# Key-key and key-query products of a delta tile made once and kept for the other scan direction

## The chip, the cores and the metric

The kernel runs on one core of one Trainium2 chip. The metric is the device time of one execution in microseconds (us), lower is better. Engines are named as the profile names them: PE (TensorE matmul), PEld (its weight load), DVE (VectorE), ACT (ScalarE), POOL (GpSimd), SP (SyncE, which issues most transfers). Numbers such as L2178 are lines of the kernel before, unless the text says "of the changed kernel".

## What is computed

One layer of a hybrid backbone: a norm and an input projection, three token mixers side by side (a gated DeltaNet, HGRN2, RG-LRU), an output projection, then a grouped top-2 mixture of 16 experts. There are 128 context tokens and 512 latent tokens. The change touches the DeltaNet alone. Cut to what matters (chunks of the reference are 64 tokens; the kernel handles two at a time, 128 tokens, and gets the same result):

```python
def _gdn_step(S, inp):
    q, k, v, la, beta = inp
    g = jnp.cumsum(la, axis=-1)
    dec = _masked_exp(incl, g[..., :, None] - g[..., None, :])
    lmat = beta[..., :, None] * jnp.einsum('bhid,bhjd->bhij', k, k) * strict   # key-key
    m = jnp.eye(CHUNK) + lmat
    sol = triangular_solve(m, rhs, lower=True, unit_diagonal=True)
    u = sol[..., :GDN_DV] - jnp.einsum('bhck,bhkv->bhcv', sol[..., GDN_DV:], S)
    attn = jnp.einsum('bhik,bhjk->bhij', q, k) * dec                           # key-query
    o = (q * eg) @ S + attn @ u
    S_new = exp(g_end) * S + (k * exp(g_end - g)).T @ u

o_a, st_a = _bidirectional(_gdn_step, s_gdn, (q, k, v, log_alpha[0], beta[0]), (q, k, v, log_alpha[1], beta[1]))
```

Both directions use the same q and k. Only the decays (`dec`) and `beta` differ by direction.

## The kernel before, in words

The 640 tokens are five tiles of 128: tile 0 is the context, tiles 1 to 4 the latents. The delta scan runs in five steps, s = 0 to 4. In each step both directions are worked side by side, four heads each, so that everything comes in eights: the forward direction takes tile `FWD[s]` (0, 1, 2, 3, 4), the backward one tile `BWD[s]` (0, 4, 3, 2, 1). So steps 1 and 4 work on the tiles 1 and 4, steps 2 and 3 on the tiles 2 and 3, with the directions exchanged, and step 0 has tile 0 in both.

The order of the work is written out by hand in `gdn_order()` (L80), and every engine walks through the same list. It is a chain of *levels* that inverts the triangular matrix of step s by doubling (`level`, l = 0 to 5, then the corner blocks `t6` and `d6`), and between the levels one group of eight products is put that belongs to the step before or after. The names of these groups are:

- `gb`: the cumulated decays of the next step (L1098). `wt`: their weighting by beta (L2157, DVE).
- `kk`, key-key products of the next step (L1100), after level 4. DVE multiplies them with the masked decays (L2223 to L2228, four products: two of 64 partitions by 512 elements, two of 64 by 256). The first two give `a_ATc`, of which POOL makes the masks of the next step.
- `kq`, key-query products of the next step (L1102), between `t6` and `d6`. DVE multiplies them with the decays (L2234, one product of 128 by 1024).
- `ks`: keys times state (L1109), after level 5; DVE makes the right side of it (L2249, L2253 twice). `u`: the solution (L1113). `ds`: the state's increment (L1115). `o`: the output (L1122, L1125).

A level is, on PE, products into PSUM (`t1`, two halves of 16 blocks of 64x64), a copy of them by ACT (L1578), products again (`dd`), and a subtraction by DVE (L2178, twice, one for each half). The next level starts with what that subtraction wrote. `level(s, 0)` is on DVE two pairs of products, L2164 (from two SBUF tiles) and L2167 (from SBUF and PSUM). DVE walks its list in order: level 4, `kk` of the next step, level 5, `ks`, `kq` of the next step, level 0 of the next step.

POOL works in order too (L1756 to L1785). For the next step it masks the decays (L1762 twice), copies the step's end decays (L1765 twice), scales queries and keys (L1771 twice, L1777 twice), and then makes six masks of `a_ATc` (L1753 six times), level by level. All of these read and write SBUF.

PSUM has four pairs of banks. The groups of eight products alternate between pairs 2 and 3 (`psum_plan`, L149), in the order of the plan; a group waits until the pair's last user has been read. SP loads rows of the modulation into `xT` after the last use of `xT` as gate weights (L644), then waits for further points of the delta scan, one after the other, before it starts the next transfers.

## Time and profile before

| | |
|---|---|
| runs | 3, median 1076.65 us (1075.40 to 1076.88) |
| span of the profiled execution | 1071.6 us |
| median of the runs less that span | 5.05 us |
| PE busy | 942.1 us (88%) |
| DVE busy | 443.8 us (41%) |
| ACT busy | 257.5 us (24%) |
| POOL busy | 134.6 us (13%) |
| delta scan, about | 427 us to 640 us of the span |

The span goes from the first to the last instruction. The record of the profiled execution has its span and not a time of its own; the 5.05 us are what the timed runs have around such a span. In the rows of a timeline the first number is the start in us from the span's start, the second the time from the first start to the last end of the instructions that the row merges; xN is how many these are; in brackets stands how long the engine was idle before, and who ended that.

### The profile page before, as it was taken

The numbers are of one execution on the slowest core, as the hardware profiler recorded it, in microseconds if no ns is written. First come the engines' busy times: TensorE is split into PE (matmuls) and PEld (weight loads), VectorE is DVE, ScalarE is ACT, GpSimd is POOL, SyncE is SP. The second block draws the span as 40 slices with busy tenths as digits, with TensorE's granted clock in tenths as the row PEclk, the third lists the DMA queues.
The fourth block names the chain that finished last, engine by engine and source line by source line (L and its number), as shares of the span: only waits on it lengthen the run. The fifth ranks groups of instructions, "written<-read, shape, count | busy, mean of one in ns | idle before, by whom it ended". The sixth has DMA issues, their size and how long they took to land.

```text
span 1071.6 us, 23772 instructions
## 1 busy us (share of the span) xinstructions
PE 942.1 (88%) x10749; PEld 655.2 (61%) x10749; DVE 443.8 (41%) x734; ACT 257.5 (24%) x436; POOL 134.6 (13%) x154
## 2 busy tenths in 40 slices
PE   2799998878999889999999799998899999999940
PEld 2554576765665446688999664565858756665510
DVE  1443767974345333465667631555100010100037
ACT  3418233233113227231322310220101101100103
POOL 4000000000003100554246000001000000000021
PEclk9899999989999999999999989988999999999985
DMA  8902008654021900200000247142589999999845
GB/s 297 382 27 79 1 1 316 238 175 147 8 78 61 339 19 1 83 19 22 2 3 23 78 179 313 60 177 94 211 304 386 398 403 383 398 394 395 347 156 195
DMA packets 55772, 192.60 MB, mean 180 GB/s; under 512 B 7323, under 2 KB 10834, under 8 KB 51570
## 3 DMA queue, kind: packets, MB, share of 16 engines
q1 hardware_dynamic: 42096, 161.09, 39.7%
q0 software_dynamic: 6736, 22.81, 6.6%
q10 hardware_dynamic: 6834, 7.11, 1.9%
q8 instruction: 87, 1.43, 0.6%
q14 instruction: 19, 0.16, 0.0%
HBM read 168.27 MB, written 22.73 MB: 178 GB/s over the span
## 4 chain that ended last, share of the span: by engine, by line
PE 74%; DVE 11%; DMA 6%; ACT 4%; issue 4%; ACTq 1%; DVEq 0%; SPq 0%; POOLq 0%
PE ps L731 16%; PE ps L1199 14%; PE ps L1222 7%; PE ps L1019 6%; PE ps L1072 6%; PE ps L721 4%; PE ps L1007 4%; PE ps L976 3%; DMA ring<-in_moe_w_up 2%; PE ps L870 2%; PE ps L821 2%; PE ps L748 2%; DMA ring<-in_ada_w 1%; PE ps L1140 1%; PE ps L967 1%
## 5 line engine op out<-in xcount | busy, mean ns | idle before, releaser
L731 PE MATMUL ps<-hT,ring 128*128 128x128 f32 x704 | 194.2, 437 | 1.9 <-ACT hT L1323 1.9
L731 PEld LDWEIGHTS ps<-hT,ring 128*128 128x128 f32 x704 | 106.8, 193 | 83.6 <-issue 80.1
L2440 DVE TENSOR_TENSOR hT<-ps,hT 128x384 f32<-128x384 f32 (+3 forms) x18 | 9.1, 506 | 245.9 <-ACT hT L1641 235.7
L1199 PE MATMUL ps<-ring,arena 128*32 128x128 f32 (+3 forms) x1104 | 87.3, 377 | 2.5 <-DMA ring<-in_moe_w_up 1.3
L1199 PEld LDWEIGHTS ps<-ring,arena 128*32 128x32 f32 (+1 forms) x1104 | 61.1, 118 | 28.5 <-issue 20.4
L1796 POOL DMA_INDIRECT arena<-h_rows,slot_tok x18 | 16.6, 922 | 384.4 <-PE ps L721 229.5
L1199 PE MATMUL ps<-arena 128*32 128x256 f32 (+2 forms) x1056 | 60.8, 387 | 4.4 <-DVE arena L2432 2.7
L1199 PEld LDWEIGHTS ps<-arena 128*32 128x32 f32 x1056 | 46.7, 112 | 19.4 <-issue 5.0
L721 PE MATMUL ps<-ident,arena 128*128 128x128 f32 (+3 forms) x316 | 44.3, 289 | 11.6 <-DVE arena L2207 5.0
L721 PEld LDWEIGHTS ps<-ident,arena 128*128 128x128 f32 (+3 forms) x316 | 39.3, 177 | 20.6 <-issue 7.7
L2178 DVE TENSOR_TENSOR arena<-arena,ps 128x512 f32<-128x512 f32 x50 | 34.4, 688 | 29.5 <-PE ps L1019 28.7
L1641 ACT ACTIVATE hT<-ps 128x384 f32<-128x384 f32 (+3 forms) x18 | 8.1, 449 | 148.8 <-PE ps L1199 148.8
L1222 PE MATMUL ps<-ring,hT 128*32 128x256 f32 (+2 forms) x384 | 41.4, 470 | 0.5 <-ACT hT L1648 0.5
L1222 PE MATMUL ps<-arena,hT 128*32 128x512 f32 (+2 forms) x360 | 39.5, 516 | 2.0 <-ACT hT L1648 2.0
L748 PE MATMUL ps<-ring,st 128*32 128x128 f32 x768 | 28.4, 309 | 13.4 <-DMA ring<-in_ada_w 6.4
L1578 ACT ACTIVATE hT<-ps 128x256 f32<-128x256 f32 x50 | 18.8, 382 | 87.7 <-PE ps L1019 82.7
L1019 PE MATMUL ps<-arena,hT 64*64 64x64 f32 x960 | 38.0, 219 | 0.2 <-DVE arena L2178 0.2
L1019 PE MATMUL ps<-hT,arena 64*64 64x64 f32 x800 | 33.0, 221 | 5.6 <-ACT hT L1578 5.3
L1072 PE MATMUL ps<-ring,hT 128*128 128x512 f32 x80 | 36.1, 594 | 0.4 <-issue 0.4
L1072 PE MATMUL ps<-ring,mixBC 128*128 128x512 f32 x80 | 36.0, 593 | 0.0
L1652 ACT ACTIVATE hT<-ps 128x768 f32<-128x768 f32 (+3 forms) x18 | 13.1, 727 | 94.5 <-PE ps L1222 94.5
L976 PE MATMUL ps<-xT,hT 128*128 128x512 f32 x80 | 34.9, 594 | 0.6 <-DVE ring L2228 0.6
(438 smaller groups left out, 1485.3 us busy)
## 6 DMA issues: line engine op xcount, KB each, us to landing
ring<-in_ada_w SPq DMA_DIRECT2D x12, 2048.0 KB, 11.3
ring<-in_moe_w_gate SPq DMA_DIRECT2D x7, 2048.0 KB, 9.9
arena<-in_moe_w_gate SPq DMA_DIRECT2D x7, 2048.0 KB, 10.7
arena<-in_moe_w_up SPq DMA_DIRECT2D x7, 2048.0 KB, 15.6
arena<-in_moe_w_down SPq DMA_DIRECT2D x7, 2048.0 KB, 20.4
ring<-in_moe_w_up SPq DMA_DIRECT2D x7, 2048.0 KB, 16.5
ring<-in_moe_w_down SPq DMA_DIRECT2D x7, 2048.0 KB, 21.9
ring<-in_w_in SPq DMA_DIRECT2D x6, 2048.0 KB, 12.8
```

Source lines behind the costliest of these rows:

```text
L721: return nc.tensor.transpose(out, in_, ident[0:n, 0:n])
L731: last = mm(out, w[:, k, cols], rhs(k)[:, a:b], start=(k == 0), stop=(k == KD - 1))
L748: last = mm(bank(name)[32 * c:32 * c + 32, 0:P], cs[:, k, :], slab(name)[:, k, P * c:P * c + P], start=(k == 0), stop=(k == KD - 1))
L821: last = mm(bank(name)[:, 0:256], hT[:, k, P * t:P * t + P], hgate_w[:, k, :], start=(k == 0), stop=(k == KD - 1))
L870: last = mm(bank(name)[64 * r:64 * r + 64, at:at + 64], lhs[:, keys:keys + 64], rhs[:, queries:queries + 64], start=True, stop=True)
L976: last = mm(bank(name)[:, 0:512], hT[:, k, P * t:P * t + P], gate_w[:, k, :], start=(k == 0), stop=(k == KD - 1))
L1007: last = mm(bank(name)[:, P * dh:P * dh + P], lhs(dh), rhs(dh), start=True, stop=True)
L1019: last = mm(out[r, 64 * h:64 * h + 64], lhs[r, 4 * g + h, :], rhs(r, 4 * g + h), start=True, stop=True)
L1072: last = mm(bank(name)[:, 0:512], mix(k, t), slab(("out", half))[:, k, :], start=(k == 0), stop=(k == KD - 1))
L1199: last = mm(ps[rows_of(n, g), GU, 512 * i + at:512 * i + at + width], m_xgT[:, b % 2, k, rows_of(n, j)], w[:, k, col:col + width], start=( ...
L1222: last = mm(ps[rows_of(n, g), DN, at:at + width], m_hidT[:, b % 2, first:first + (P if n == 4 else 32)], w[:, f, col:col + width], start=( ...
L2178: TT(out=XX, in0=XX, in1=bank(name)[:, 0:512].rearrange("p (a x) -> p a x", a=2), op=SUB).then_inc(pair_free[pair(name)], 1)
```

## The change

`kk` and `kq` are made on PE in the steps 0, 1 and 2 only. Step 0 makes four products instead of eight, and DVE reads these four for both directions, from PSUM as before. In the steps 1 and 2 all eight are made, and ACT copies them from PSUM into two buffers in `xT` (`a_kk`, `a_kq`: four tiles, four heads, 128 each). From step 1 on DVE reads them there, in the steps 3 and 4 with the directions exchanged. Two new semaphores take the place of the PSUM pair's, and SP's load of the modulation's rows into `xT` now waits for the last use of the two buffers.

```diff
+LAST_PAIR = 2
@@ job_plan
+        elif kind in ("kk", "kq") and s > LAST_PAIR:
+            continue
@@ layer_program
+        a_kk, a_kq = (xTf[:, 2048 * n:2048 * n + 2048].rearrange("p (n h t) -> p n h t", n=NT - 1, h=GH) for n in range(2))
+        def both_ways(kept, s):
+            return kept[:, FWD[s] - 1::NT - 2 * s][:, 0:2]
@@ SP
-                    sp.wait_ge(*full_after(LATE_GATES[-1]))
+                    sp.wait_ge(s_a_kk_used, NT - 1)
+                    sp.wait_ge(s_a_kq_used, NT - 1)
@@ PE
-                    pe.wait_ge(*free_after(("kk", s)))
+                    pe.wait_ge(*(s_a_kk_used, s) if s else free_after(("kk", 0)))
...
-                    eight(name, kT(s), kT(s))
+                    if s <= LAST_PAIR:
+                        eight(name, kT(s), kT(s), 8 if s else 4)
...
-                    eight(name, kT(s), qT(s))
+                    if s <= LAST_PAIR:
+                        eight(name, kT(s), qT(s), 8 if s else 4)
@@ ACT
+                elif kind in ("kk", "kq") and 0 < s <= LAST_PAIR:
+                    act.wait_ge(*full_after(LATE_GATES[-1]))
+                    act.wait_ge(*full_after(name))
+                    A(both_ways(a_kk if kind == "kk" else a_kq, s), bank(name).rearrange("p (d h t) -> p d h t", d=2, h=GH),
+                      ACT.Copy).then_inc(pair_free[pair(name)], 1)
@@ DVE
+            def pair_products(name, kept):
+                s = name[1]
+                if s == 0:
+                    dve.wait_ge(*full_after(name))
+                    return wide(fours_of(bank(name)[:, 0:512]), 1, 2)
+                for n in range(1, min(s, LAST_PAIR) + 1):
+                    dve.wait_ge(*free_after((name[0], n)))
+                return both_ways(kept, s)
...
-                    dec, kk = a_dec[s % 2], eight(bank(name))
-                    dve.wait_ge(*full_after(name))
+                    dec, kk = by_way(a_dec[s % 2]), pair_products(name, a_kk)
...
-                    ch(TT(out=a_ATc[lower, :, :], in0=kk[lower, :, 0:64], in1=dec[lower, :, 0:64], op=MULT))
+                    ch(TT(out=by_way(a_ATc)[lower], in0=kk[lower, :, :, 0:64], in1=dec[lower, :, :, 0:64], op=MULT))
...
-                    TT(out=a_dec[s % 2], in0=eight(bank(name)), in1=a_dec[s % 2], op=MULT).then_inc(pair_free[pair(name)], 1)
+                    TT(out=dec, in0=kq, in1=dec, op=MULT).then_inc(s_a_kq_used if s else pair_free[pair(name)], 1)
```

How instructions stand now is shown at three places. The first is PE at the end of step 2, from the last products of level 4 on, where `kk`, `ks`, `kq` stood between the levels' small products; L1007 is `kk`, `ks` and `kq` in that order, L1051 is `t6` and `d6`, the last row is level 0 of step 3. Before:

```order
L1019 MATMUL ps<-arena,hT 64x64 x8
L1007 MATMUL ps<-arena 128x128 x8
L1019 MATMUL ps<-arena,hT 64x64 x16
L1019 MATMUL ps<-hT,arena 64x64 x8
L1019 MATMUL ps<-arena,hT 64x64 x8
L1019 MATMUL ps<-hT,arena 64x64 x8
L1019 MATMUL ps<-arena,hT 64x64 x8
L1007 MATMUL ps<-arena 128x128 x8
L1051 MATMUL ps<-arena,ring 64x64 x8
L1007 MATMUL ps<-arena 128x128 x8
L1051 MATMUL ps<-arena,hT 64x64 x8
L1019 MATMUL ps<-ident,arena 64x64 x16
```

The same place of the changed kernel, where L1019 is now the groups of eight, L1031 the levels' products, L1063 `t6` and `d6`:

```order
L1031 MATMUL ps<-arena,hT 64x64 x24
L1031 MATMUL ps<-hT,arena 64x64 x8
L1031 MATMUL ps<-arena,hT 64x64 x8
L1031 MATMUL ps<-hT,arena 64x64 x8
L1031 MATMUL ps<-arena,hT 64x64 x8
L1019 MATMUL ps<-arena 128x128 x8
L1063 MATMUL ps<-arena,ring 64x64 x8
L1063 MATMUL ps<-arena,hT 64x64 x8
L1031 MATMUL ps<-ident,arena 64x64 x16
```

`kk` and `kq` are gone, so level 5 follows on level 4 and `d6` on `t6` with no product between; `ks` is the one group of eight left. The second place is DVE at the same time, from level 4 of step 2 to `kq` of step 3. Before:

```order
L2178 TENSOR_TENSOR arena<-arena,ps 128x2x256 [waits bank_free3,bank_full3]
L2223 TENSOR_TENSOR arena<-ps,hT 64x512 [waits a_ct,a_tri,pair_full2]
L2224 TENSOR_TENSOR arena<-ps,hT 64x512
L2227 TENSOR_TENSOR ring<-ps,hT 64x256 [waits bank_full0]
L2228 TENSOR_TENSOR ring<-ps,hT 64x256
L2178 TENSOR_TENSOR arena<-arena,ps 128x2x256 [waits bank_free2,bank_full2]
L2178 TENSOR_TENSOR arena<-arena,ps 128x2x256 [waits bank_free3,bank_full3]
L2249 TENSOR_TENSOR ring<-ps,arena 128x1024 [waits pair_full2,pair_full3]
L2253 TENSOR_TENSOR ring<-arena,ring 128x512 [waits pair_free3]
L2253 TENSOR_TENSOR ring<-arena,ring 128x512
L2234 TENSOR_TENSOR hT<-ps,hT 128x1024 [waits pair_free2,a_pk,pair_full2]
```

The same place of the changed kernel:

```order
L2209 TENSOR_TENSOR arena<-arena,ps 128x2x256 [waits bank_free3,bank_full3]
L2253 TENSOR_TENSOR arena<-xT,hT 64x512 [waits a_tri,a_ct,pair_free3,pair_free2]
L2254 TENSOR_TENSOR arena<-xT,hT 64x512
L2257 TENSOR_TENSOR ring<-xT,hT 64x256 [waits bank_full0]
L2258 TENSOR_TENSOR ring<-xT,hT 64x256
L2209 TENSOR_TENSOR arena<-arena,ps 128x2x256 [waits bank_free2,bank_full2]
L2209 TENSOR_TENSOR arena<-arena,ps 128x2x256 [waits bank_free3,bank_full3]
L2279 TENSOR_TENSOR ring<-ps,arena 128x1024 [waits pair_full2]
L2283 TENSOR_TENSOR ring<-arena,ring 128x512 [waits pair_free2]
L2283 TENSOR_TENSOR ring<-arena,ring 128x512
L2264 TENSOR_TENSOR hT<-xT,hT 128x1024 [waits a_pk,a_kk_used,pair_free3,pair_free2]
```

The instructions and their order are the same. What changed is the first input of the four `kk` products and of the `kq` product, `xT` in SBUF instead of `ps` in PSUM, and what they wait for. The third place is SP after the narrow router load; before, the first of these transfers waits for the last gate products (L644). Of the changed kernel:

```order
L636 DMA xT<-modulation_rows 128x1024 [waits a_kk_used,a_kq_used,z_stored,rows_stored]
L636 DMA xT<-scale_rows 128x1024
L636 DMA xT<-modulation_rows 128x1024
L636 DMA xT<-scale_rows 128x1024
L636 DMA xT<-modulation_rows 128x1024
L636 DMA rows_w<-modulation_rows 128x1024 [waits a_ct]
```

The five loads into `xT` now wait for `kq` of step 4 on DVE. The next one waits, as before, for the masks of step 4.

## Rows read from the trace of the kernel before

**Rows 1.** The page: busy time by engine, and the chain's shares by engine.
```profile
PE 942.1 (88%) x10749; PEld 655.2 (61%) x10749; DVE 443.8 (41%) x734; ACT 257.5 (24%) x436; POOL 134.6 (13%) x154
...
PE 74%; DVE 11%; DMA 6%; ACT 4%; issue 4%; ACTq 1%; DVEq 0%; SPq 0%; POOLq 0%
```

**Rows 2.** Busy time by stretch: stretch, its length, PE, PEld, DVE, ACT, POOL, clock, DMA.
```profile
514.00:548.00 34.00, 33.77 (x677) 31.82 (x676) 22.61 (x31) 8.99 (x18) 15.45 (x14) 1.00 0.01 3
...
616.00:640.00 24.00, 23.43 (x93) 15.12 (x94) 6.56 (x10) 4.44 (x6) 0.00 (x0) 0.88 0.57 204
```

**Rows 3.** Timeline, PE, in the steps 2 and 4.
```profile
535.61 2.05 PE L1007 MATMUL ps<-arena 128*128 128x128 f32 x16
...
550.00 0.68 PE L1019 MATMUL ps<-arena 64*64 64x64 f32 x16 [0.42 <-DVE arena L2167]
...
594.43 0.68 PE L1019 MATMUL ps<-arena 64*64 64x64 f32 x16 [0.20 <-DVE arena L2178]
```

**Rows 4.** Timeline, DVE, from level 4 of step 2 to level 0 of step 3.
```profile
534.96 1.45 DVE L2178 TENSOR_TENSOR arena<-arena,ps 128x512 f32<-128x512 f32 x2 [0.18 <-DVE arena L2279]
537.70 0.68 DVE L2223 TENSOR_TENSOR arena<-ps,hT 64x512 f32<-64x512 f32 x1 [1.28 <-PE ps L1007]
...
540.05 0.69 DVE L2178 TENSOR_TENSOR arena<-arena,ps 128x512 f32<-128x512 f32 x1
...
542.86 1.23 DVE L2249 TENSOR_TENSOR ring<-ps,arena 128x1024 f32<-128x1024 f32 x1 [1.28 <-PE ps L1007]
544.12 2.53 DVE L2253 TENSOR_TENSOR ring<-arena,ring 128x512 f32<-128x512 f32 x2
546.57 1.21 DVE L2234 TENSOR_TENSOR hT<-ps,hT 128x1024 f32<-128x1024 f32 x1
...
549.45 0.41 DVE L2167 TENSOR_TENSOR arena<-identc,ps 128x256 f32<-128x256 f32 x1
```

**Rows 5.** Timeline, POOL, the same stretch.
```profile
536.23 2.49 POOL L1771 TENSOR_TENSOR hT<-hT,arena 128x512 f32<-128x512 f32 x2
538.68 2.05 POOL L1777 TENSOR_TENSOR hT<-arena,hT 128x512 f32<-128x512 f32 x2
540.69 7.09 POOL L1753 TENSOR_TENSOR arena<-arena,rows_w 128x512 f32<-128x512 f32 x5
547.74 1.50 POOL L1753 TENSOR_TENSOR hT<-arena,rows_w 128x512 f32<-128x512 f32 x1
```

**Rows 6.** By line: count, ns of one (min/median/max), first and last start.
```profile
L2253 DVE TENSOR_TENSOR ring<-arena,ring x10: 684/1461/1804, 473.1 to 611.6; 128x512 f32<-128x512 f32 x10
```

**Rows 7.** The same view, of POOL's masks.
```profile
L1753 POOL TENSOR_TENSOR arena<-arena,rows_w x25: 1262/1272/1726, 442.0 to 580.2; 128x512 f32<-128x512 f32 x25
```

**Rows 8.** The same view, of the products of level 0.
```profile
L2164 DVE TENSOR_TENSOR arena<-identc,arena x10: 407/507/1475, 443.3 to 582.5; 128x256 f32<-128x256 f32 x10
```

**Rows 9.** Timeline, ACT, a copy of eight products out of PSUM.
```profile
516.75 1.02 ACT L1600 ACTIVATE hT<-ps 128x1024 f32<-128x1024 f32 x1
```

**Rows 10.** Timeline, DVE and POOL, around `kk` of step 1.
```profile
465.53 2.49 POOL L1771 TENSOR_TENSOR hT<-hT,arena 128x512 f32<-128x512 f32 x2
...
466.69 0.68 DVE L2223 TENSOR_TENSOR arena<-ps,hT 64x512 f32<-64x512 f32 x1 [1.28 <-PE ps L1007]
...
478.76 0.41 DVE L2167 TENSOR_TENSOR arena<-identc,ps 128x256 f32<-128x256 f32 x1
```

**Rows 11.** Timeline, DVE and POOL, around `kk` of step 2.
```profile
502.10 2.05 POOL L1777 TENSOR_TENSOR ring<-arena,ring 128x512 f32<-128x512 f32 x2
503.24 0.68 DVE L2223 TENSOR_TENSOR arena<-ps,ring 64x512 f32<-64x512 f32 x1 [1.28 <-PE ps L1007]
...
515.19 0.41 DVE L2167 TENSOR_TENSOR arena<-identc,ps 128x256 f32<-128x256 f32 x1
```

**Rows 12.** Timeline, DVE, the first use of the modulation's rows in `xT`.
```profile
629.48 0.69 DVE L2184 TENSOR_TENSOR arena<-ps,xT 128x512 f32<-128x512 f32 x1 [12.97 <-PE ps L1072]
```

**Rows 13.** Transfers of 444 to 460 us: issue, KB each, us to landing.
```profile
xT<-modulation_rows SPq DMA_DIRECT2D x3, 512.0 KB, 7.1
```

More of the change, by code:

```diff
@@ L406, in layer_program @@
         s_a_la = sem("a_la")
+        s_a_kk_used = sem("a_kk_used")
+        s_a_kq_used = sem("a_kq_used")
         s_a_ln = sem("a_ln")
@@ L1001, in _, with eight @@
             pe.wait_ge(s_a_norm, 2)
-            def eight(name, lhs, rhs):
+            def eight(name, lhs, rhs, n=8):
                 pe.wait_ge(*free_before(name))
-                for dh in range(8):
+                for dh in range(n):
                     last = mm(bank(name)[:, P * dh:P * dh + P], lhs(dh), rhs(dh), start=True, stop=True)
@@ L1116, in _ @@
                 elif kind == "o":
-                    pe.wait_ge(*free_after(("kq", s)))
+                    pe.wait_ge(*(s_a_kq_used, s) if s else free_after(("kq", 0)))
                     pe.wait_ge(s_a_pk, s + 1)
@@ L2142, in _ @@
             fours_of = lambda v: v.rearrange("p (a b) -> p a b", a=GH)
+            by_way = lambda v: v.rearrange("p (d h) t -> p d h t", d=2)
+            def pair_products(name, kept):
[6 more added lines that the diff above has]
+                return both_ways(kept, s)
             def decays(s):
@@ L2222, in _ @@
                         dve.wait_ge(s_a_ct, 6 * s)
-                    ch(TT(out=a_ATc[lower, :, :], in0=kk[lower, :, 0:64], in1=dec[lower, :, 0:64], op=MULT))
-                    TT(out=a_ATc[upper, :, :], in0=kk[upper, :, 64:P], in1=dec[upper, :, 64:P], op=MULT).then_inc(s_a_atc, 1)
+                    ch(TT(out=by_way(a_ATc)[lower], in0=kk[lower, :, :, 0:64], in1=dec[lower, :, :, 0:64], op=MULT))
+                    TT(out=by_way(a_ATc)[upper], in0=kk[upper, :, :, 64:P], in1=dec[upper, :, :, 64:P], op=MULT).then_inc(s_a_atc, 1)
                     if s >= 2:
                         dve.wait_ge(*full_after(("t6", s - 2)))
-                    ch(TT(out=a_CT6[s % 2][lower, :, :], in0=kk[lower, 0:4, 64:P], in1=dec[lower, 0:4, 64:P], op=MULT))
-                    TT(out=a_CT6[s % 2][upper, :, :], in0=kk[upper, 4:8, 0:64], in1=dec[upper, 4:8, 0:64],
-                       op=MULT).then_inc(pair_free[pair(name)], 1)
+                    ch(TT(out=a_CT6[s % 2][lower, :, :], in0=kk[lower, 0, :, 64:P], in1=dec[lower, 0, :, 64:P], op=MULT))
+                    TT(out=a_CT6[s % 2][upper, :, :], in0=kk[upper, 1, :, 0:64], in1=dec[upper, 1, :, 0:64],
+                       op=MULT).then_inc(s_a_kk_used if s else pair_free[pair(name)], 1)
                 elif kind == "kq":
-                    dve.wait_ge(*full_after(name))
+                    dec, kq = by_way(a_dec[s % 2]), pair_products(name, a_kq)
                     dve.wait_ge(s_a_pk, s + 1)
-                    dve.wait_ge(*free_after(("kk", s)))
-                    TT(out=a_dec[s % 2], in0=eight(bank(name)), in1=a_dec[s % 2], op=MULT).then_inc(pair_free[pair(name)], 1)
+                    dve.wait_ge(*(s_a_kk_used, s) if s else free_after(("kk", 0)))
+                    TT(out=dec, in0=kq, in1=dec, op=MULT).then_inc(s_a_kq_used if s else pair_free[pair(name)], 1)
                 elif kind == "level":
```

## The prediction

> **What bounds the kernel now.** I read the page's busy times first, then its chain. PE is busy 942.1 us of 1071.6, and the chain that ended last runs on PE for 74% of its time and on DVE for 11% [rows 1]. So work taken from PE may pay, but only where PE is what is waited for. The view by stretch says that PE is hardly ever at rest in a step of the delta scan: 33.77 of 34.00 us, with DVE busy 22.61 and POOL 15.45 [rows 2]. The timelines show why the share misleads. The chain of a step is PE, ACT, PE, DVE, level by level, and the groups of eight products fill what PE would otherwise wait. One such group takes 2.05 us [rows 3]. In step 4, where a gap holds no group, PE waits 0.20 us for DVE's subtraction and goes on [rows 3]. So a group taken out between two levels is worth 2.0 less 0.2, 1.8 us, if DVE has nothing more to do there.
>
> At the end of a step it is not PE that bounds. From level 5 on, DVE works without a pause: L2249 starts at 542.86, the two L2253 follow, then `kq`'s L2234, then level 0, whose last product starts at 549.45 and ends at 549.86 [rows 4]. PE waits for that last one and starts level 1's second half at 550.00 [rows 3]. Whatever makes this row of DVE instructions longer moves every later step, and with them all the rest.
>
> The third thing to see is how DVE and POOL get in each other's way. L2253 reads two SBUF tiles. It takes 0.68 us at least, but 1.46 in the median and 1.80 at most [rows 6]. POOL's masks take 1.27 and up to 1.73 [rows 7]. L2164, also from two SBUF tiles, takes 0.41 to 1.48 [rows 8]. In the same stretch L2234 (1.21 for 1024 elements), L2223 (0.68) and L2178 (0.69), each with one input in PSUM, are not stretched, though POOL is busy from 536.23 to 549.24 without a gap [rows 4, 5]. So a DVE product of two SBUF tiles and a POOL instruction run one after the other. The maxima fit strict turns: 1.80 is about one POOL instruction of 1.2 and DVE's own 0.55, and 1.73 is DVE's 0.55 and POOL's 1.17.
>
> The Trainium skill says the same on its page "SBUF — State Buffer", section "Who interferes with whom": a VectorE instruction with two SBUF inputs contends with a GpSimd instruction that reads SBUF, one with at most one does not. No row here shows such a product on 64 partitions, as four of the five touched ones are; the page makes no exception for them.
>
> **The change, part by part.** Times are those of the trace before, held still up to the point of the change.
>
> *Products taken from PE.* Eight calls in step 0 and 16 each in the steps 3 and 4, 40 in all, at 2.05/8 = 0.26 us each: 10.3 us of PE time. Of that only `kk` of the steps 3 and 4 stands between two levels, worth at most 2 x 1.8 = 3.6 us. `kq` stands where DVE bounds (PE waits at 550.00), so I count 0 for it; the other bound is 2 x 2.0.
>
> *Step 0.* Four products less before DVE's first `kk` product: between 0 and 1.0 us. DVE also waits there for POOL's masked decays, so I take 0.3, near the lower end.
>
> *The first input in SBUF.* Five DVE products in each of the steps 1 to 4 now have two SBUF inputs, just while POOL works. To go through them I use, from [rows 6 to 8]: once POOL's instruction ends, a waiting DVE product needs 0.55 us (512 elements), 0.28 (256, from 1.48 less 1.2) or 1.1 (1024; estimate, twice the first); then the waiting POOL instruction runs, 1.13 to 1.17, or 0.9 for L1777 (2.05 for two [rows 5]).
>
> Step 3: DVE ends level 4 at 536.41 [rows 4] and needs no PE product now, so `kk` can start. POOL began L1771 at 536.23 [rows 5]. Turns: POOL ends at 537.50, DVE's first `kk` product 538.05; POOL 539.2, second 539.75; L1777 540.65, third 540.95; L1777 541.85, fourth 542.15. Before, level 5's subtraction came right behind at 540.05 [rows 4]; now it ends for both halves at 543.55. PE's `ks` is done long before. L2249 runs 543.6 to 544.8 (before it started at 542.86, so the gain on PE has turned into a loss of 0.7). POOL's masks go on from 542.15: 543.25, 544.45, 545.7. First L2253 to 546.25, mask to 547.4, second to 547.95, mask to 549.1, `kq` to 550.2, last mask to 551.5. Then level 0: L2164 0.3, L2167 0.3, and the same again with POOL at rest, until 552.8. Before it was 549.86: **+2.95 us**, with the gain of the missing `kk` group inside. Step 4 has the same spacing: **+2.95**.
>
> Step 1: here ACT copies first, 1.02 us a copy [rows 9]. DVE's `kk` starts at 467.75 instead of 466.69, while POOL, begun at 465.53 [rows 10], is in its second L1771. Turns: 468.6, 470.05, 471.2, 472.65; level 5 ends at 474.1; L2249 475.35; first L2253 waits for the third mask behind it and ends at 476.8, the second at 478.5, `kq` behind the last mask at 480.9; level 0 ends at 482.3 with POOL at rest. Before: 478.76 + 0.41 = 479.17 [rows 10]. **+3.15**. ACT's copy of `kk` also holds up level 5's copies by some 0.4 us, that of `kq` the two of `d6` by some 0.5; both lie under DVE's delay.
>
> Step 2: the copy ends at 504.25, when POOL has just ended L1777 (502.10 + 2.05) and waits for `a_ATc` [rows 11]. So the first two products run free, and the masks start about 1.0 later than before. By the same turns level 5 ends at about 508.8, `kq` near 515.7 and level 0 near 517.1, against 515.60 before: **+1.5**.
>
> *Queues and transfers.* Behind the waiting `kk` product on DVE stand level 5's subtractions, and PE's `t6` waits for these: that is the path counted. On SP five loads of 512 KB move from 447 us to behind `kq` of step 4, about 590 to 595. They landed in about 7.1 us each, overlapping [rows 13]; at the 204 GB/s of a busy stretch [rows 2] 2.6 MB take 13 us. Behind them on SP stand the last row and the inputs' rows, which wait for later points anyway. The first reader is at 629.48 [rows 12]: over 20 us in hand, cost 0. The turns of pairs 2 and 3 shift by two in the steps 3 and 4, always with a released one: 0.
>
> *Sum:* -0.3 + 3.15 + 1.5 + 2 x 2.95 = +10.25 us. The profiled span would be 1071.6 + 10.25 = 1081.9; with the 5.05 us around it, the runs' median 1076.65 becomes **1086.9**. Nothing behind the scan has slack that takes it back, since out-projection and experts start from its end.
>
> **Rivals.**
>
> *The products do not collide* (64 partitions, or DVE gets through before POOL's next instruction). Then the steps 3 and 4 gain 1.8 each, the steps 1 and 2 lose 0 to 0.5 by ACT's copy (DVE's `kk` 1.1 later, but `ks` on PE covers most of it), step 0 gains 0.3: 1076.65 - 3.9 + 0.5 = 1073.3. Against it stand [rows 6 to 8], where all products of two SBUF tiles that meet POOL grow. This is the one on the other side. It decides at the length of the first `kk` product in step 3: under about 0.8 us, the change wins.
>
> *PE's time is what counts*: 10.3 us less, 1066.4. The Trainium skill, "Perfetto Trace Analysis", section "Identifying the Most-Contended Engine", would have the engine with the highest occupancy optimized first, which is PE here; the wait at 550.00 speaks against it at this place.
>
> *Turns, but milder.* If one in two products gets through free, each step loses half of the 0.55 + 1.15 turns, and the steps 3 and 4 about break even: about 1080.5.
>
> *The clock falls as well.* PE now has rests of about 2 us at `t6`, `u` and level 1 of the steps 3 and 4. In 616 to 640 us, behind a longer rest, the granted clock was 0.88 on average, a share of 0.24 of the stretch at 1.2 instead of 2.4 GHz [rows 2]: 5.8 us at half speed, 2.9 us lost. One such loss in each of the four steps makes 1086.9 + 11.6 = 1098.5, one in all 1089.8. In the scan before, the clock was 1.00, with PE never at rest for long.
>
> *The rows come late*: five loads would have to take over 30 us. No row speaks for it.
>
> **How the numbers follow.** Turns as worked out 0.68 (1083 to 1091); clock falls too 0.09 (1089 to 1098); milder turns 0.10 (1077 to 1083); no collision 0.09 (1073.3); PE's time 0.02 (1066.4); the rest 0.02. What a measurement of this kernel can tell from no change is about 0.2%, 2.2 us. Faster: 0.09 + 0.02 = 0.11. Same: the lower edge of the milder case and strays, 0.05. Slower: 0.84. The range leaves out the two faster cases below and the worst of the clock above: 1078.5 to 1094.
>
> **What would show it.** In the steps 3 and 4 the `kk` products with `xT` as input should take 1.5 to 1.8 us (512) and about 1.2 to 1.5 (256), `kq` about 2.2 to 2.4 instead of 1.21, POOL's L1771, L1777 and masks should grow as well, PE should rest behind `ks` for `t6` about 2 us, and these two steps should be about 3 us longer than before. I am wrong if the `kk` products stay at 0.69 and 0.42, if PE starts level 1 at once behind `u`, or if a gap opens at the first reader of the modulation's rows.

## The result, and the profile after

The changed kernel takes 1088.35 us (median of 20 runs, 1082.22 to 1092.08), the kernel before 1077.93 (20 runs, 1070.12 to 1086.35). The ratio is 1.0089, with a 95% interval of 1.0066 to 1.0112: 9.6 us slower, with 7.1 to 12.1 as the interval (the medians themselves are 10.4 apart). The ratios here and below leave out runs more than 1.5% above the fastest of their kernel, such as four of the 23 runs of the kernel before in the second group of experiments, so a ratio can differ from that of the medians. Predicted were 1086.9 us and +10.25. The profiled execution of the changed kernel has a span of 1088.8 us and took 1090.58.

The page after, busy times and chain; it stands against [rows 1]:

```profile
PE 946.5 (87%) x10669; PEld 658.7 (60%) x10669; DVE 459.5 (42%) x734; ACT 261.4 (24%) x440; POOL 140.0 (13%) x154
...
PE 71%; DVE 13%; issue 5%; ACT 5%; DMA 4%; ACTq 1%; POOL 0%; DVEq 0%; SPq 0%; POOLq 0%
```

PE has 80 records less (40 calls, two records each) and is busy longer all the same. DVE has as many instructions as before and is busy 15.7 us more, POOL 5.4 more. That is the first sign: work was taken from one engine, and the two others pay by length, not by count.

Busy time by stretch, columns as in [rows 2]:

```profile
514.00:548.00 34.00, 32.03 (x666) 30.03 (x668) 25.39 (x30) 9.86 (x20) 13.44 (x11) 1.00 0.01 3
548.00:582.00 34.00, 29.67 (x570) 27.83 (x566) 25.68 (x27) 8.57 (x17) 15.95 (x11) 0.90 0.01 2
```

The timeline of DVE from level 4 of step 2 to level 0 of step 3, the place of [rows 4]. L2253 to L2258 are `kk`, L2264 is `kq`, L2209 a level's subtraction, L2279 and L2283 `ks`, L2195 and L2198 level 0:

```profile
545.71 1.45 DVE L2209 TENSOR_TENSOR arena<-arena,ps 128x512 f32<-128x512 f32 x2 [0.18 <-DVE arena L2309]
547.19 1.59 DVE L2253 TENSOR_TENSOR arena<-xT,hT 64x512 f32<-64x512 f32 x1
548.82 1.65 DVE L2254 TENSOR_TENSOR arena<-xT,hT 64x512 f32<-64x512 f32 x1
550.50 1.16 DVE L2257 TENSOR_TENSOR ring<-xT,hT 64x256 f32<-64x256 f32 x1
551.69 1.16 DVE L2258 TENSOR_TENSOR ring<-xT,hT 64x256 f32<-64x256 f32 x1
552.88 1.29 DVE L2209 TENSOR_TENSOR arena<-arena,ps 128x512 f32<-128x512 f32 x2
554.08 1.22 DVE L2279 TENSOR_TENSOR ring<-ps,arena 128x1024 f32<-128x1024 f32 x1
555.34 3.32 DVE L2283 TENSOR_TENSOR ring<-arena,ring 128x512 f32<-128x512 f32 x2
558.58 2.28 DVE L2264 TENSOR_TENSOR hT<-xT,hT 128x1024 f32<-128x1024 f32 x1
560.79 1.49 DVE L2195 TENSOR_TENSOR arena<-identc,arena 128x256 f32<-128x256 f32 x1
562.20 0.41 DVE L2198 TENSOR_TENSOR arena<-identc,ps 128x256 f32<-128x256 f32 x1
...
562.87 0.41 DVE L2198 TENSOR_TENSOR arena<-identc,ps 128x256 f32<-128x256 f32 x1
```

POOL in the same stretch, the place of [rows 5]; L1790 and L1796 are the scalings, L1772 the masks:

```profile
546.98 2.94 POOL L1790 TENSOR_TENSOR hT<-hT,arena 128x512 f32<-128x512 f32 x2
549.89 2.68 POOL L1796 TENSOR_TENSOR hT<-arena,hT 128x512 f32<-128x512 f32 x2
552.53 7.25 POOL L1772 TENSOR_TENSOR arena<-arena,rows_w 128x512 f32<-128x512 f32 x5
559.75 2.25 POOL L1772 TENSOR_TENSOR hT<-arena,rows_w 128x512 f32<-128x512 f32 x1
```

From the end of level 4 to the end of level 0, DVE needed 13.45 us before (536.41 to 549.86). Now it is 547.16 to 563.28, 16.12 us, with no rest between. The step became longer by that difference. PE waits behind the row, as the rows of its timeline that have a wait say:

```profile
554.42 0.83 PE L1063 MATMUL ps<-arena,ring 64*64 64x64 f32 x16 [2.68 <-DVE arena L2209]
...
558.71 3.43 PE L1019 MATMUL ps<-ring,arena 128*128 128x128 f32 x16 [0.52 <-DVE ring L2283]
562.75 1.35 PE L1031 MATMUL ps<-arena 64*64 64x64 f32 x32 [0.61 <-DVE arena L2198]
```

The group of eight at 558.71 took 2.05 us at the full clock and takes 3.43 here, since the granted clock fell from 2.4 to 1.2 GHz behind the rest (0.90 on average in the stretch). It costs little: it ends at 562.14, when DVE still has level 0 to finish (563.28), and PE then waits 0.61 us for DVE.

To see where the time went, I measured each step of the scan from the end of level 1's second subtraction to the same point of the next step. For the last boundary of the kernel after these are the two rows here (603.55 less 566.73):

```profile
566.04 0.69 DVE L2209 TENSOR_TENSOR arena<-arena,ps 128x512 f32<-128x512 f32 x1 [0.25 <-PE ps L1031]
...
602.86 0.69 DVE L2209 TENSOR_TENSOR arena<-arena,ps 128x512 f32<-128x512 f32 x1 [0.25 <-PE ps L1031]
```

In the table, "into step n" holds the end of step n-1 with the `kk` and `kq` of step n, the prediction's "Step n". All are us, from one profiled execution each; the two marked "again" are from the experiments below.

| kernel | into 1 | into 2 | into 3 | into 4 | sum | rest of the span |
|---|---|---|---|---|---|---|
| before | 30.24 | 36.57 | 34.12 | 34.14 | 135.07 | 936.5 |
| before, again | 30.24 | 38.11 | 34.14 | 34.15 | 136.64 | 939.7 |
| after | 33.66 | 39.45 | 36.83 | 36.82 | 146.76 | 942.0 |
| after, again | 33.33 | 39.45 | 36.82 | 36.99 | 146.59 | 935.6 |

So the four steps cost 10.0 to 11.7 us. The rest of the span differs by 3.2 us between the two executions of the kernel before and by 6.4 between the two of the changed kernel.

### The profile page after: what moved, and what is told of

The parts are those of the page before. It is cut to its first block, busy times and chain, and to the rows that moved or that the text cites. A ratio compares the mean times of both kernels' runs of the same rounds, so it can differ in the third digit from the quotient of the medians.

```text
span 1088.8 us, 23627 instructions
## 1 busy us (share of the span) xinstructions
PE 946.5 (87%) x10669; PEld 658.7 (60%) x10669; DVE 459.5 (42%) x734; ACT 261.4 (24%) x440; POOL 140.0 (13%) x154
## 4 chain that ended last, share of the span: by engine, by line
PE 71%; DVE 13%; issue 5%; ACT 5%; DMA 4%; ACTq 1%; POOL 0%; DVEq 0%; SPq 0%; POOLq 0%
PE ps L743 16%; PE ps L1213 14%; PE ps L1236 7%; PE ps L1084 6%; PE ps L1031 6%; PE ps L733 4%; PE ps L1019 3%; PE ps L988 3%; PE ps L833 2%; PE ps L882 2%; DMA ring<-in_moe_w_gate 2%; PE ps L760 1%; PE ps L1154 1%; DMA ring<-in_ada_w 1%; PE ps L979 1%
## 5 line engine op out<-in xcount | busy, mean ns | idle before, releaser
L733 PE MATMUL ps<-ident,arena 128*128 128x128 f32 (+3 forms) x316 | 46.7, 299 | 12.3 <-DVE arena L2238 5.0
L733 PEld LDWEIGHTS ps<-ident,arena 128*128 128x128 f32 (+3 forms) x316 | 41.7, 183 | 19.7 <-issue 6.4
L2209 DVE TENSOR_TENSOR arena<-arena,ps 128x512 f32<-128x512 f32 x50 | 34.0, 687 | 32.8 <-PE ps L1031 32.0
L1031 PE MATMUL ps<-arena,hT 64*64 64x64 f32 x960 | 40.2, 226 | 0.5 <-issue 0.3
L1031 PE MATMUL ps<-hT,arena 64*64 64x64 f32 x800 | 34.0, 226 | 6.4 <-ACT hT L1592 6.2
L1236 PE MATMUL ps<-arena,hT 128*32 128x512 f32 (+2 forms) x360 | 36.2, 490 | 2.0 <-ACT hT L1667 2.0
L1031 PEld LDWEIGHTS ps<-arena,hT 64*64 64x64 f32 x960 | 35.0, 142 | 1.5 <-issue 0.8
```

The source lines that it names most:

```text
L733: return nc.tensor.transpose(out, in_, ident[0:n, 0:n])
L1031: last = mm(out[r, 64 * h:64 * h + 64], lhs[r, 4 * g + h, :], rhs(r, 4 * g + h), start=True, stop=True)
L1236: last = mm(ps[rows_of(n, g), DN, at:at + width], m_hidT[:, b % 2, first:first + (P if n == 4 else 32)], w[:, f, col:col + width], start=( ...
L2209: TT(out=XX, in0=XX, in1=bank(name)[:, 0:512].rearrange("p (a x) -> p a x", a=2), op=SUB).then_inc(pair_free[pair(name)], 1)
```

## The experiments

Eleven runs of ten kernels follow, in three groups. Each group ran on one chip, with runs of the kernel before beside it. My theory: the cost is the five DVE products that now read two SBUF tiles while POOL works. The rivals: ACT's copies, the lower clock, the rest on PE, the place of the row loads.

**The products back in PSUM.** `kk` is kept in SBUF as in the change, but in the steps 3 and 4 ACT copies it back into PSUM, where DVE reads it; `kq` is as before the change.

```diff
 ACT, behind wt of the steps 3 and 4
+    A(bank(("kk", s)).rearrange("p (d h t) -> p d h t", d=2, h=GH), both_ways(a_kk, s),
+      ACT.Copy).then_inc(pair_full[pair(("kk", s))], 1)
 ACT, behind ks of the steps 0 and 1
+    n = ("kk", s + 1)
...
+    A(both_ways(a_kk, s + 1), bank(n).rearrange("p (d h t) -> p d h t", d=2, h=GH),
+      ACT.Copy).then_inc(s_a_kept, 1)
 PE
-    eight(name, kT(s), kT(s))
+    if s <= LAST_PAIR:
+        eight(name, kT(s), kT(s), 8 if s else 4)
 SP, ahead of the five loads of rows
-    sp.wait_ge(*full_after(LATE_GATES[-1]))
+    sp.wait_ge(*full_after(("kk", NT - 1)))
```

> The kernel before, with the key-key half of the change made another way: kk is not made on PE in the steps 3 and 4 (four products in step 0), ACT keeps the tiles of the steps 1 and 2 in SBUF after DVE has read them in PSUM, and copies them back into the PSUM pair early in the steps 3 and 4, so that DVE's first input is in PSUM in every step. kq stays on PE in all steps. Theory (turns between DVE and POOL over two SBUF inputs are the whole loss): the kk products stay at 0.68 and 0.42 us, level 5 of the steps 2 and 3 follows level 4 at once, these two steps are about 1.8 us shorter than before, the steps 0 and 1 as before: about 3.6 us under the kernel before, ratio 0.9965. Rival (the loss comes from PE's rests and the lower clock, or from the copies): the kernel is no faster than before, or slower by 2 us and more.

Measured: 1072.64 us (12 runs), ratio to before 0.9935 (0.9904 to 0.9966). Its DVE, at the same place; L2247 to L2252 are `kk`:

```profile
537.43 0.68 DVE L2247 TENSOR_TENSOR arena<-ps,hT 64x512 f32<-64x512 f32 x1
538.13 0.69 DVE L2248 TENSOR_TENSOR arena<-ps,hT 64x512 f32<-64x512 f32 x1
538.86 0.42 DVE L2251 TENSOR_TENSOR ring<-ps,hT 64x256 f32<-64x256 f32 x1
539.31 0.43 DVE L2252 TENSOR_TENSOR ring<-ps,hT 64x256 f32<-64x256 f32 x1
539.77 1.28 DVE L2200 TENSOR_TENSOR arena<-arena,ps 128x512 f32<-128x512 f32 x2
```

The same four products, with the same POOL work beside them (its scalings run from 537.33 to 541.84), take 0.68 and 0.42 us instead of 1.6 and 1.16. For these four only the first input's memory differs. ACT's copy stands in a gap:

```profile
532.61 1.03 ACT L1594 ACTIVATE ps<-xT 128x1024 f32<-128x1024 f32 x1
```

The steps took 30.24, 36.58, 32.91 and 34.14 us: the step into 3 is 1.2 shorter than before, where 1.8 was forecast. At `ks` DVE is 1.83 us ahead (from the start of level 4 to `ks` it is 6.07 us instead of 7.90), but its next two products, which read two SBUF tiles in both kernels, now meet POOL for longer and take 3.13 us, where [rows 4] have 2.53:

```profile
543.39 3.13 DVE L2277 TENSOR_TENSOR ring<-arena,ring 128x512 f32<-128x512 f32 x2
```

The step into 4 is not shorter. There the trace of PE shows a pause inside `ks` whose end no semaphore explains:

```profile
573.73 0.72 PE L1014 MATMUL ps<-arena 128*128 128x128 f32 x5
576.27 0.72 PE L1014 MATMUL ps<-arena 128*128 128x128 f32 x5 [1.82 <-issue]
```

**POOL holds back.** POOL begins its scalings only when DVE has done `kk`; all else is the changed kernel.

```diff
                 pool.wait_ge(s_a_tri, 2 * s + 2)
+                if s:
+                    pool.wait_ge(s_a_kk_used, s)
```

> The changed kernel, with one wait more: POOL scales queries and keys of a step only after DVE has gone through that step's four kk products, so that these no longer meet a POOL instruction. Theory: the kk products fall from 1.15 to 1.7 us to 0.69 and 0.42, POOL's chain starts 2.3 us later, kq (also two SBUF inputs) stays at about 2.3 us; the steps 0, 2 and 3 come out 1 to 2.5 us shorter than in the changed kernel, 1081 to 1086 in all. Rival (it is not the port): the kk products keep their length or the steps theirs, and the later POOL chain makes it slower than the changed kernel.

Measured: 1079.8 us (10 runs), ratio 1.0007 (0.9978 to 1.0036); steps 32.22, 38.59, 36.08, 35.16. That is below the 1081 to 1086 that were forecast, though the steps are only 0.7 to 1.7 us shorter than in the changed kernel. DVE, POOL and PE into step 3, one fence each:

```profile
543.98 0.68 DVE L2255 TENSOR_TENSOR arena<-xT,hT 64x512 f32<-64x512 f32 x1
544.69 0.69 DVE L2256 TENSOR_TENSOR arena<-xT,hT 64x512 f32<-64x512 f32 x1
545.41 0.42 DVE L2259 TENSOR_TENSOR ring<-xT,hT 64x256 f32<-64x256 f32 x1
```

```profile
551.39 7.95 POOL L1772 TENSOR_TENSOR arena<-arena,rows_w 128x512 f32<-128x512 f32 x5
```

```profile
553.15 1.98 PE L1031 MATMUL ps<-ident,arena 64*64 64x64 f32 x32 [2.84 <-POOL arena L1772]
```

This is the cleanest proof of the mechanism: the same instructions with the same SBUF inputs take 0.68 and 0.42 us once POOL is silent (it rests 2.77 us there). Part of the gain is lost again, since the masks come later and PE now waits 2.84 us for the first of them; the granted clock is also at half there, from about 552 to 559 us.

**One of the two products alone.** First `kk` alone, then `kq` alone; the other is as before the change.

```diff
-        elif kind in ("kk", "kq") and s > LAST_PAIR:
+        elif kind == "kk" and s > LAST_PAIR:
```

> The changed kernel with kq undone: kq made on PE in every step and read from PSUM; kk as in the changed kernel. Theory: kq falls from 2.3 to 1.2 us, the masks behind it end earlier only in part, so each of the four steps is 0.5 to 1.2 us shorter than in the changed kernel: 1083 to 1086, still 5 to 8 us over the kernel before. PE has one rest less (kq fills it), so the clock should stay at the full level more often. Rival (kq carries most of the loss): within 2 us of the kernel before.

Measured: 1080.84 us (10 runs), ratio 1.001 (0.9981 to 1.0039); steps 33.55, 38.45, 35.98, 36.08. The total is below the 1083 to 1086 of the forecast, and the clock fell in each step all the same. The `kk` products are as long as in the change. `kq`, from PSUM, is 1.21 again while POOL's masks run:

```profile
547.19 1.71 DVE L2251 TENSOR_TENSOR arena<-xT,hT 64x512 f32<-64x512 f32 x1
...
558.70 1.21 DVE L2262 TENSOR_TENSOR hT<-ps,hT 128x1024 f32<-128x1024 f32 x1
```

> Only the key-query products are kept, the key-key products are made by PE in every step and read from PSUM as before. By the turns with POOL: kq takes 2.28 us instead of 1.21 where a mask runs beside it (the steps 2, 3 and 4), about 1.3 in step 1; the kk products take 0.68 and 0.42. So three of the four steps are 1.0 to 1.3 us longer than before, some of that given back by masks that end earlier relative to DVE, and the total is +2 to +4 us, 1080 to 1082 beside a kernel before of 1078. If the losses of kk and kq were separate and added up, kq's share would be this and kk's the rest of 9.6 us, but the run with kk alone was only 0 to 4 above: so a rival is that kq_only costs 6 us or more.

Measured: 1081.04 us (10 runs), ratio 1.0034 (0.9999 to 1.007); steps 32.91, 38.41, 36.91, 35.73. Into step 3:

```profile
551.41 2.29 DVE L2263 TENSOR_TENSOR hT<-xT,hT 128x1024 f32<-128x1024 f32 x1
553.62 1.48 DVE L2193 TENSOR_TENSOR arena<-identc,arena 128x256 f32<-128x256 f32 x1
```

`kq` is 1.08 longer, but it collides in the steps 1, 3 and 4 and not in step 2 (1.21 there), where I had expected step 1 to be the free one. Behind it level 0 has two products of two SBUF tiles. In the kernel before the second of them met POOL's last mask, now the first does, so together they are 0.32 longer (1.48 and 0.41 instead of 0.41 and 1.16):

```profile
547.70 0.41 DVE L2164 TENSOR_TENSOR arena<-identc,arena 128x256 f32<-128x256 f32 x1
...
548.37 1.16 DVE L2164 TENSOR_TENSOR arena<-identc,arena 128x256 f32<-128x256 f32 x1
```

So the collision costs 1.40 us a step, near my 1.0 to 1.3. The step into 3 is 2.8 longer than before all the same, since the clock fell right behind: from 558 to 561 us it was 0.59 on average, and from the end of level 0 to the end of level 1 it took 4.80 us instead of 3.42. To keep the two apart, here is DVE's row alone, from the end of level 4 to the end of level 0, as the 13.45 and 16.12 above (us, from the timelines of DVE):

| kernel | step 1 | step 2 | step 3 | step 4 | over before |
|---|---|---|---|---|---|
| before | 13.76 | 13.65 | 13.45 | 13.45 | |
| after | 16.57 | 15.09 | 16.12 | 16.12 | 9.6 |
| after, again | 16.58 | 15.70 | 16.10 | 16.12 | 10.2 |
| `kk` alone | 16.01 | 14.08 | 15.15 | 15.13 | 6.1 |
| `kq` alone | 15.15 | 13.66 | 14.85 | 14.85 | 4.2 |

The two shares add up to about the whole. What the steps of these two kernels have beyond the rows is mostly the clock at half speed in levels 1 and 4: their steps sum to 7.4 and 7.3 more than those of the second profile of before. The total of `kq` alone, +3.7, is where I expected it and agrees with its rows. That of `kk` alone, +1.1 and at most 4.2 by its interval, is too small for its rows, and its profiled execution was the slowest of its ten. The same holds for all four kernels of the first group (the products back in PSUM, POOL holds back, `kk` alone, ACT copies in all steps): their totals lie 4 to 6 us below what their steps give against the second profile of before. What made this offset, common to a group measured on one chip, no run shows.

**ACT copies in all steps.** PE makes `kk` and `kq` in every step, ACT copies each to SBUF.

```diff
-LAST_PAIR = 2
+LAST_PAIR = 4
 ACT, ahead of each copy
+                    if s > 2:
+                        act.wait_ge(s_a_kk_used if kind == "kk" else s_a_kq_used, s - 1)
```

> The changed kernel with LAST_PAIR = 4: PE makes kk and kq in every step, ACT copies them in every step, DVE reads SBUF. So it has the SBUF inputs and the copies and none of the saved PE products except those of step 0. Theory: the saved kk group of PE was worth something only as an earlier start of DVE's kk (2.4 us earlier in the steps 2 and 3 of the scan's list), most of which the turns with POOL eat; each of these two steps is 1 to 2.5 us longer than in the changed kernel, 1090 to 1094 in all. Rival (PE's products count fully, 2 us for each of four groups): 1096 or more. Rival (they count nothing): as the changed kernel.

Measured: 1086.26 us (10 runs), ratio 1.005 (1.0022 to 1.0078); steps 33.09, 39.47, 38.06, 37.25, sum 147.87. The total is below the 1090 to 1094 of the forecast; the steps into 3 and 4 are 1.2 and 0.4 longer than in the changed kernel, where 1 to 2.5 was forecast. With almost all of PE's work still there the scan is about 1 us slower than the change's, so the loss does not come from taking work from PE. But two things make it here. In the step into 3 DVE's first `kk` product starts 2.90 us behind level 4, when ACT's copy has landed, instead of 1.28, and the four products take 0.96, 1.43, 0.42 and 1.38 us, 2.0 more than from PSUM.

**The rest on PE filled.** Eight products that nobody reads, in the rest behind `ks`.

```diff
+                    if s + 1 < NT:
+                        for _ in range(8):
+                            mm(ps[:, 0, 256:384], ident[:, :], ones[:, :], start=True, stop=True)
```

> The changed kernel with eight products of 128x128 whose results nobody reads, put on PE where it rests behind ks of the steps 0 to 3. They add 2.05 us of PE time to each rest of 2.7. If the granted clock has a share in the loss, the drops to half speed at 554 and 592 us are gone and the time is 2 to 5 us below the changed kernel's 1088.3, at 1083 to 1086. If the row of DVE products alone sets the end of a step, the steps stay at 33.7, 39.4, 36.8 and 36.8 us within 0.5, less up to 1.4 where the second had a drop in level 4, and the time is 1087 to 1089. In both cases the kk products stay at 1.6 and 1.16 us and kq at 2.28.

Measured: 1088.4 us (4 runs), ratio 1.0104 (1.004 to 1.0168); steps 33.09, 38.32, 36.81, 36.83. At 554 us the clock is full, at 589 it falls again. The steps into 3 and 4 are those of the changed kernel to 0.02 us, with 2.05 us of PE work more in each and another clock: there DVE's row sets the end. The step into 2 is 1.1 shorter, with the clock full in level 4 of step 1. The steps sum to 145.05, 1.5 to 1.7 less than in the two profiles of the changed kernel: so the lower clock costs about that much, if the eight products change nothing else. The products themselves cost some in step 0 (1.5), and behind step 4 PE has a pause of 2.20 us beside the row loads (issued from 591.68), so the total can't tell the clock's share:

```profile
602.57 0.27 PE L1142 MATMUL ps<-hT 128*128 128x128 f32 x1 [2.20 <-issue]
```

**The row loads later.** As the first experiment, with the five loads of rows behind level 0 of step 4.

```diff
+                    sp.wait_ge(s_a_ct, 6 * NT)
```

> The key-key products are copied back into PSUM as in the run psum_copy_back, and the five loads of rows start only behind level 0 of step 4 (after about 583 us). Theory: the PE pause of 1.8 us inside ks of step 3, for which the profile shows no releaser, comes from the five loads that run beside it; then it is gone, step 3 takes 32.3 to 32.9 us like step 2 instead of 34.1, and the whole 1 to 1.5 us less than psum_copy_back, 1071 to 1072. Rival: the pause is there by chance or has another reason; then it stays or turns up elsewhere, and the time is that of psum_copy_back, 1072.6 within 1.5.

Measured: 1072.87 us (12 runs), ratio 0.9958 (0.9926 to 0.999); steps 30.23, 36.59, 32.90, 32.91. The step into 4 is short now, as the theory had it. But the pause has moved with the loads, which SP issues from 583.67 on:

```profile
595.90 0.62 PE L1027 MATMUL ps<-arena,hT 64*64 64x64 f32 x13 [1.44 <-issue]
```

From the last step to the first reader of the rows it took 44.83 us instead of 41.89, 1.44 of it this pause, so the step's gain was given back at once. The total did not fall to the 1071 to 1072 of the forecast. In the kernel with `kq` alone the loads start at 590.87 and the pause (1.29) ends at 601.79; with ACT's copies in all steps it is 601.14, and 1.53 ending at 614.92. It thus ends 10 to 14 us after the first load in each, and so does the one in the kernel with the filled rest. The control below loads its rows from 575.89, near the place of the first experiment, and has no such pause. What PE's queue waits for there the profile does not say.

**The same kernels again, and a control.** A second profile of before and of after, a control for the first experiment, and the first experiment again.

> The kernel before, unchanged, profiled a second time, since its first profiled execution was quicker than the median of its runs. If the change's cost sits in the rows of the steps alone, the four boundaries between steps are 30.2, 36.6, 34.1 and 34.1 us again, the product of kq takes 1.21 us and the first kk product 0.68 us; a longer span must then come from stretches outside the scan, at a lower granted clock. The rival: the steps themselves vary between executions by a microsecond or more, and part of the difference that I read between the two kernels' profiles is this spread.

Measured: 1078.06 us, steps in the table. Three repeat to 0.02 us, the one into step 2 is 1.54 longer: the clock fell in level 4 of step 1, as it did at this place in both profiles of the changed kernel. PE before, again:

```profile
503.95 0.94 PE L1019 MATMUL ps<-hT,arena 64*64 64x64 f32 x16 [2.12 <-ACT hT L1578]
504.68 1.07 PE L1019 MATMUL ps<-arena,hT 64*64 64x64 f32 x16
505.53 1.07 PE L1019 MATMUL ps<-hT,arena 64*64 64x64 f32 x16
```

> The changed kernel profiled a second time, because the second profile of the kernel before showed that one step varies by 1.5 us with the granted clock. If the DVE row sets the steps, they are 33.7, 38 to 39.5, 36.8 and 36.8 us again, with kk at 1.6 and 1.16 us and kq at 2.28, and where the clock is full in level 4 of step 1 the second step is 38.0. If what I took for turns was spread between executions, the steps differ by a microsecond or more from those of the first profile.

Measured: 1083.9 us. The steps repeat to 0.33 us, `kk` takes 1.60, 1.65, 1.16, 1.16 and `kq` 2.28 again.

The control keeps all of the first experiment except the reuse: PE makes `kk` of the steps 3 and 4 anew.

```diff
-                    if s <= LAST_PAIR:
-                        eight(name, kT(s), kT(s), 8 if s else 4)
+                    eight(name, kT(s), kT(s), 8 if s else 4)
 ACT, behind wt of the steps 3 and 4
-    A(bank(("kk", s)).rearrange("p (d h t) -> p d h t", d=2, h=GH), both_ways(a_kk, s), ACT.Copy)
```

> As psum_copy_back (ACT keeps the key-key products of the steps 1 and 2 in SBUF, step 0 makes four products, the five row loads start behind kk of step 4), but PE makes the products of the steps 3 and 4 anew and nothing is copied back. Theory: what psum_copy_back gained is the two groups of kk taken from between two levels, 1.2 us each where no fetch pause gives it back; then this kernel is that much slower than psum_copy_back and its steps are 30.2, 36.6, 34.1 and 34.1. By the profiles the two groups are worth 1.2 to 2.5 us, and the medians differed by 7: the rival is that most of the 7 us comes from something else that both kernels share (the place of the row loads, or the four products less in step 0), and then this kernel too is at 1073 to 1076, with a ratio to before of 0.995 to 0.998.

> The run psum_copy_back again, beside copy_no_reuse on the same chip: ratio to before 0.990 to 0.997 if the gain is real, 1071 to 1075 us. Theory for its profile: steps 30.2, 36.6, 32.9 and 34.1 us, a PE pause of 1 to 2 us with no releaser somewhere beside the five loads at 566 to 577 us. If the pause is not there, the last step is 32.9 too.

Measured: the control 1076.9 us (12 runs), ratio 0.9998 (0.9961 to 1.0034), steps 30.24, 36.58, 34.14, 34.13. The first experiment again: 1074.7 us (10 runs), ratio 0.9958 (0.992 to 0.9996), steps 30.23, 38.11, 32.90, 35.74, with the pause once more (2.09, ending at 579.65; loads from 569.74) and a clock drop at 580. The control is the kernel before to 0.02 us in its steps, and in time no difference shows, so ACT's keeping copies, which stand behind DVE's reading here, and the later loads cost the steps nothing. What the first experiment gains in its steps is the missing `kk` of two steps, 1.2 us each where no pause gives it back. Against the kernel before it is 0.42 and 0.65%, 4.5 and 7 us; against the control, beside it on one chip, the medians are 2.2 us apart, which 12 and 10 runs that each spread over 11 us do not settle. The profiles explain 1.2 to 2.5 us, and what the larger figures hold beyond that stays open. By its ratio this is the best version that I ran.

## Why the prediction was right

*What bounds a step.* Right. The row of DVE instructions grew by 2.67 us and the step into 3 by 2.71. PE lost a group and rests 2.68 us instead; filled or empty, this rest does not change the steps into 3 and 4.

*The turns.* Right, and in their sizes too: in the steps 3 and 4 1.59 to 1.71 for the 512-element products (forecast 1.5 to 1.8), 1.16 for 256 (1.2 to 1.5, so 0.04 below), 2.28 for `kq` (2.2 to 2.4). They hold for 64 partitions. Two experiments take the collision away from either side, PSUM for one input or POOL silent, and both bring back 0.68 and 0.42.

*The terms.* DVE's rows grew by 2.81, 1.44, 2.67 and 2.67 us in the steps 1 to 4, against forecasts of 3.15, 1.5, 2.95 and 2.95: each a little less (in the second profile step 2 is 2.05, where ACT's copy came 0.6 later, and the others are the same). The steps themselves: "Step 1" +3.42 and +3.09, where the row is +2.8 in both profiles and the rest goes with half the clock (0.59 from 479 to 483 us). "Step 2" +1.34 against the profile of before with the same clock drop in level 4, +2.88 against the one without. "Step 3" and "Step 4" +2.69 and +2.67 to +2.84. In the steps 1 and 2 the turns are not all of it: DVE's first `kk` product starts 2.40 and 2.45 us behind level 4 instead of 1.28 and 1.29, which is ACT's copy, as forecast, and what that alone costs was not measured. "Step 0" -0.3: DVE's first `kk` product comes 3.90 us after `wt` instead of 4.14, so 0.24 were gained; but the `kq` product behind it waits for POOL's scalings, and comes 8.72 after `wt` where it was 8.74. From `wt` to level 1 it is 18.98 to 18.99 in all four profiles: 0. The sum was +10.25. The rows give +9.6 and +10.2, the steps +9.95 to +10.1 against the second profile of before, the ratio of the runs +9.6 (7.1 to 12.1). That the total came so near is in part luck: the four rows were up to 1.0 us below their terms, the gain of "Step 0" did not come, and the clock, which had no term, added up to 1.7, while the rest of the span varies by 3 to 6 us between executions.

*What was off.* "The 5.05 us around the span" was wrong as a thing: the profiled run of the changed kernel has 1.78 us around its span (1090.58 less 1088.8), those of the other kernels 1.7 to 2.0. The other 3.3 were a quick profiled execution of before, 1073.4 us. The addition came out right, since the difference to the median was what was needed. A group of eight between two levels was priced at 1.8 us, in the steps 3 and 4 and in the rival without collision; the products back in PSUM gave 1.2, since DVE's later products of two SBUF tiles took 0.6 of it back. I also had nothing for the stretch from the last step to the first reader of the rows. It took 44.12 and 42.74 us against 42.06 and 42.19 before. Of the 1.93 us between 44.12 and 42.19, 1.25 is one group of eight products at half clock (3.33 against 2.08) and 0.28 a pause of PE beside the row loads. These loads come well before their reader, at 647.67, as forecast.

*The rivals.* "No collision" fell with the first `kk` product. "PE's time is what counts" fell with the change's own steps. "Milder turns" fell with the steps 3 and 4, where all five products grew. Only where ACT's copy had made DVE late did some get through: the first of step 1 (0.75 us, started at 472.25, when POOL's first scalings were about to end at 472.46), and the first three of step 2 (0.68, 0.69, 0.42), where I had foreseen two. "The clock falls as well" was right in the event and wrong in the price. In both profiles of the changed kernel it fell once in each step, at 479, 507, 554 and 592 us in the first, where the first profile of before has it full up to 614. The rival had 2.9 us for each. At 554 and 592 it lies beneath DVE's row and costs next to nothing; from the end of level 0 to the end of level 1 of step 1 it took 4.03 and 3.69 us where the filled rest had 3.45, and level 4 of step 1 cost up to 1.5. With the rest filled, the four steps were 1.5 to 1.7 us shorter in all, not 11.6. The prediction's sentence that PE is never at rest for long in the scan before was wrong as well, and this wait of the kernel before is the one behind which its second profile has the drop:

```profile
499.14 0.68 PE L1019 MATMUL ps<-hT,arena 64*64 64x64 f32 x16 [2.12 <-ACT hT L1578]
```

On its page "SBUF — State Buffer", section "Who interferes with whom", the Trainium skill names exactly this pair. By that rule both cures follow: one input from PSUM, or GpSimd silent. The runs agree with each, 0.68 instead of 1.6 us.

## What to carry to other kernels

Work taken from the busiest engine pays only where that engine is waited for, and the memory that a kept result lies in is part of its price. Before a product is kept in SBUF, look at which engine reads it next, whether its other input lies in SBUF too, and whether POOL works at that time; if so, let an idle ACT put it back into PSUM. To judge a change of 1%, compare the lengths of the same steps in two profiles: they repeat to some hundredths of a microsecond where the clock is the same, while whole runs of one kernel vary by 10 to 16 us.

## What the runs showed of the hardware

- The time of a run goes with its mean granted clock. Over 80 of the 81 runs of the kernel before beside the experiments (without the one of 1414.75 us, at a clock of 0.66) the correlation is -0.92, and 0.01 of clock goes with 10.6 us; the median clock was 0.950, and 0.943 for 20 runs of the changed kernel. Which of the two drives the other is not shown by this.
- A drop of the clock can hit or miss at one place. In level 4 of step 1, behind PE's wait of 2.12 us, it came in one of two profiles of the kernel before and cost 1.54 us.
- Five loads of 512 KB beside busy PE go with a pause of 1.3 to 2.2 us in PE's issue, 10 to 14 us after the first, in six of the profiled executions, and with 0.28 and 0.26 in the two of the changed kernel. There is none with `kk` alone (loads from 589.02), where POOL holds back (591.45), in the control (575.89), and in the kernel before (447). That it moved when the loads were moved speaks for a link; its cause, and why some executions are spared, is open.
